# Constants multiplied into the next bank in TensorE's waits, and one-column sums put between dense products

## The reference, cut to what matters

```python
q = q * lax.rsqrt(jnp.sum(q * q, -1, keepdims=True) + L2_EPS)      # the one-column sums
k = k * lax.rsqrt(jnp.sum(k * k, -1, keepdims=True) + L2_EPS)
...
kk = jnp.einsum('bhnik,bhnjk->bhnij', k, k)
sol = lax.linalg.triangular_solve(amat, rhs, left_side=True, lower=True, unit_diagonal=True)
...
o = o * lax.rsqrt(jnp.mean(o * o, -1, keepdims=True) + RMS_EPS) * dn_norm_w * jax.nn.silu(z)   # the tail of a head
...
s = jnp.einsum('bqhgd,bkhd->bhgqk', qb, k, preferred_element_type=jnp.float32) * scale
p = jax.nn.softmax(s, axis=-1)
return jnp.einsum('bhgqk,bkhd->bqhgd', p.astype(v.dtype), v)
...
gu = hn @ w_ffn_in[l]
...
h = h + (jax.nn.silu(g) * u) @ w_ffn_out[l]
```

## Time and profile before

| | us |
|---|---|
| median of 3 runs | 2188.93 (2186.38 to 2196.76) |
| profiled execution | 2186.67 |
| its span | 2184.8 |
| TensorE busy | 1991.2 (91%) |
| VectorE busy | 951.7 (44%) |
| ScalarE busy | 654.0 (30%) |
| GpSimd busy | 434.0 (20%) |
| mean granted clock | 0.945 |

### The profile page before, as it was taken

One profiled execution on the slowest core, in us unless ns is written; L12 is line 12 of the kernel. 1 busy time (PEld: TensorE's weight loads), 2 busy tenths in 40 slices (PEclk: granted clock), 3 DMA queues, 4 the chain that ended last, 5 costly groups with the idle time before them and its releaser, 6 DMA issues.

```text
span 2184.8 us, 22949 instructions
## 1 busy us (share of the span) xinstructions
PE 1991.2 (91%) x9520; PEld 1442.1 (66%) x9520; DVE 951.7 (44%) x1382; ACT 654.0 (30%) x981; POOL 434.0 (20%) x310
## 2 busy tenths in 40 slices
PE   7999989999999889787787889998879899999999
PEld 5887878888877733332333347676746687888787
DVE  7674475542535622110111155845635883222332
ACT  4554422424333101000000133352226753222221
POOL 5432131423326011111110022311003120000121
PEclk9898999999999889898998999999979899999999
DMA  4861423123244589999999953111201134232210
GB/s 164 258 158 49 97 58 78 39 77 57 60 149 182 201 326 405 403 406 407 407 409 411 417 202 116 39 49 49 68 29 39 39 126 154 95 98 98 96 58 39
DMA packets 97654, 361.02 MB, mean 165 GB/s; under 512 B 9850, under 2 KB 34588, under 8 KB 85256
## 3 DMA queue, kind: packets, MB, share of 16 engines
q1 hardware_dynamic: 86800, 335.14, 42.9%
q0 software_dynamic: 8240, 19.00, 2.5%
q10 hardware_dynamic: 2504, 5.35, 0.7%
HBM read 338.74 MB, written 29.10 MB: 168 GB/s over the span
## 4 chain that ended last, share of the span: by engine, by line
PE 78%; DVE 11%; ACT 5%; issue 4%; DMA 1%; POOL 0%; ACTq 0%; SPq 0%; DVEq 0%; POOLq 0%
PE ps L272 74%; PE ps L276 3%; DVE ST L256 2%; PE ps L2080 2%; DVE H L262 1%; ACT ST L268 1%; ACT L268 1%; DVE WL L256 1%; DVE BG L262 1%; DVE ST L994 1%; ACT M L268 1%; DVE sm L3017 0%; DVE BG L256 0%; DMA BG<-h1d,toki 0%; DVE ML L256 0%
## 5 line engine op out<-in xcount | busy, mean ns | idle before, releaser
L272 PE MATMUL ps<-XH,WS 128*128 128x512 f32 x704 | 218.7, 392 | 0.0
L272 PE MATMUL ps<-HTH,WL 128*128 128x512 f32 x448 | 180.0, 402 | 0.0
L272 PE MATMUL ps<-W,BG 128*64 128x512 f32 x496 | 160.2, 618 | 1.0 <-issue 1.0
L272 PEld LDWEIGHTS ps<-XH,WS 128*128 128x128 f32 x704 | 133.5, 190 | 28.1
L2187 DVE COPY BG<-ps 128x512 f32<-128x512 f32 x32 | 22.1, 692 | 288.7 <-PE ps L272 288.7
L266 ACT ACTIVATE BG<-ps 128x512 f32<-128x512 f32 x48 | 28.5, 595 | 373.5 <-PE ps L2080 339.9
L272 PE MATMUL ps<-XL,WS 128*128 128x512 f32 x352 | 138.3, 393 | 1.8 <-DVE XL L256 1.8
L272 PE MATMUL ps<-M,BG 128*64 128x512 f32 (+1 forms) x304 | 125.9, 559 | 7.3 <-ACT ST L266 7.3
L272 PE MATMUL ps<-X2H,GV 128*128 128x512 f32 (+1 forms) x512 | 129.6, 344 | 0.0
L272 PE MATMUL ps<-ST,BG 128*64 128x512 f32 (+2 forms) x416 | 102.5, 597 | 23.5 <-issue 22.7
L272 PE MATMUL ps<-WS,HH 128*128 128x512 f32 x352 | 109.5, 393 | 2.6 <-issue 2.6
(11 more groups left out here) (394 smaller groups left out, 4443.3 us busy)
## 6 DMA issues: line engine op xcount, KB each, us to landing
W<-in_w SPq DMA_DIRECT2D x31, 2048.0 KB, 39.0
W<-in_w_in SPq DMA_DIRECT2D x27, 2048.0 KB, 9.9
ST<-in_w SPq DMA_DIRECT2D x21, 2048.0 KB
BG<-in_w SPq DMA_DIRECT2D x11, 2048.0 KB
U<-in_w SPq DMA_DIRECT2D x11, 2048.0 KB, 33.3
M<-in_w SPq DMA_DIRECT2D x11, 2048.0 KB, 37.8
HT<-in_w SPq DMA_DIRECT2D x11, 2048.0 KB
W<-in_w_ffn_in SPq DMA_DIRECT2D x22, 1024.0 KB, 7.7
```

The lines of the kernel that those rows point to most:

```text
L272: return p.e.matmul(o, lhsT=l, rhs=r, start=start, stop=stop, skip_group_check=True)
```

## The change

It consists of three kinds of edits.

1. A new helper `occupy(t, n)` issues n plain float32 products of constants (`ones` by the first 256 columns of `cst`) into tile t, whose bank has just been waited for. The real products that come next start the tile anew, so that nothing of them is left. It stands after `room(t)` and ahead of the wait for the data, and where the data's wait came first it is moved behind. Calls: 8 at d0, 8 at `x0` of heads 0 and 2, 12 at `p_v2` m=4, 8 at each of granules r6 and s5, 2 at each of the eight turns of attention heads 6 and 7, 5 at the last `p_turn3`, 3 at the first tile of `p_ffn_in`, 4 at the start of `p_ffn_out`: 80 in all.
2. `p_sums` becomes `p_sum(r, y, bank)`, a quarter of it (four products). The quarters stand after d3, d4, d5 (two), d7, d8, d9 (two), and for r=2 and 3 behind k=1 to 4 within d18 and d22.
3. The tail of head h-2 is moved within head h on all engines: the sums on TensorE from behind `kb` to behind `kk`, and into another bank (2 or 5); the scaling from behind `at` to a step behind `eg` (bank 3 or 6); on VectorE each part one step later, and `v_tail` to just ahead of the substitution rows; on ScalarE `s_tail` behind the exponential of `C`.

```diff
+        def occupy(t, n):
+            for _ in range(n):
+                mm(t.at[:, 0:256], ones, cst[:, 0:256])
...
-        def p_dense(n, bank, rhs, kind):
-            p.wait_ge(*split_done(("d", n)))
+        def p_dense(n, bank, rhs, kind, between=()):
             t = B.tile(("d", n), bank, nr=2 if n < 24 else 1)
             room(t)
+            if n == 0:
+                occupy(t, 8)
+            p.wait_ge(*split_done(("d", n)))
             x, hi, lo = parts(("d", n))
...
                 z = exact(t.at, (hi[:, k, :], lo[:, k, :]), (rhs[0][:, k, :], rhs[1][:, k, :]), k == 0, k == 7)
+                if k in between:
+                    p_sum(*between[k])
                 if k == 3:
...
-        def p_sums(r, bank):
-            t = B.tile(("nc", r), bank)
-            room(t)
-            for y in range(4):
-                m = 4 * r + y
-                p.wait_ge(sq_done, m + 1)
-                for i in range(NT):
-                    z = mm(t.at[:, 4 * i + y:4 * i + y + 1], sq_at(m)[:, i * P:(i + 1) * P], ones[:, 0:1])
-            z.then_inc(t.filled)
+        def p_sum(r, y, bank):
+            if y == 0:
+                room(B.tile(("nc", r), bank))
+            t, m = B["nc", r], 4 * r + y
+            p.wait_ge(sq_done, m + 1)
+            for i in range(NT):
+                z = mm(t.at[:, 4 * i + y:4 * i + y + 1], sq_at(m)[:, i * P:(i + 1) * P], ones[:, 0:1])
+            if y == 3:
+                z.then_inc(t.filled)
...
+        SUMS_AFTER = {3: [(0, 0)], 4: [(0, 1)], 5: [(0, 2), (0, 3)], 7: [(1, 0)], 8: [(1, 1)], 9: [(1, 2), (1, 3)]}
         def p_qk():
...
                     p_prep1()
-                    p_sums(0, 6)
                 elif n == 9:
                     p_prep2()
-                    p_sums(1, 7)
+                for r, y in SUMS_AFTER.get(n, ()):
+                    p_sum(r, y, 6 + r)
             p_beta(1, 6)
...
-        def p_turn4(key, bank, x):
+        def p_turn4(key, bank, x, n=0, ready=None):
             t = B.tile(key, bank)
             room(t)
+            if ready:
+                occupy(t, n)
+                p.wait_ge(*ready)
             for c in range(4):
...
             p_spread(("kb", h), b0, h, btr[h // 4])
-            if h > 1:
-                p_tail_sums(h - 2)
             yield
...
             p_products(("kk", h), b0 + 1, lambda c: k4[:, c, :], lambda c: Y[:, c, :])
+            if h > 1:
+                p_tail_sums(h - 2)
             p.wait_ge(gm_done, h + 1)
...
             p_products(("at", h), b0, lambda c: k4[:, c, :], lambda c: q4[:, c, :])
+            yield
+            p_spread(("eg", h), b0 + 2, h, eGr)
+            yield
             if h > 1:
                 p_tail_scale(h - 2)
-            yield
-            p_spread(("eg", h), b0 + 2, h, eGr)
-            yield
             for _ in range(8):
                 yield
-            p.wait_ge(xt0_done, h + 1)
-            p_turn4(("x0", h), b0 + 1, XT)
+            if h == 0 or h == 2:
+                p_turn4(("x0", h), b0 + 1, XT, 8, (xt0_done, h + 1))
+            else:
+                p.wait_ge(xt0_done, h + 1)
+                p_turn4(("x0", h), b0 + 1, XT)
             yield
...
         def p_tail_sums(h):
-            t, z = B.tile(("on", h), 4 + 3 * (h % 2)), sets[h % 2][3]
+            t, z = B.tile(("on", h), 2 + 3 * (h % 2)), sets[h % 2][3]
             room(t)
...
         def p_tail_scale(h):
-            t = B.tile(("os", h), 4 + 3 * (h % 2))
+            t = B.tile(("os", h), 3 + 3 * (h % 2))
             room(t)
...
             tt(v, Y, k4, four(t.at), MUL).then_inc(t.drained)
+            yield
             if h > 1:
                 v_tail_sums(h - 2)
-            yield
-            if h > 1:
-                v_tail_spread(h - 2)
             yield
...
             if h > 1:
-                v_tail(h - 2)
+                v_tail_spread(h - 2)
             yield
...
             yield
+            if h > 1:
+                v_tail(h - 2)
             for i0, i1 in ((1, 5), (5, 8), (8, 10), (10, 12), (12, 14), (14, 15), (15, DB)):
...
             LT, C, X, XT, Y, AT = sets[h % 2]
-            if h > 1:
-                s_tail(h - 2)
             yield
...
             act(C, four(t.at), ACT.Exp).then_inc(t.drained)
-            for _ in range(11):
+            yield
+            if h > 1:
+                s_tail(h - 2)
+            for _ in range(10):
                 yield
...
             for n in range(12, 24):
-                half = p_dense(n, n % 2, hTp, "T")
-                next(half)
-                yield
-                if n == 18 or n == 22:
-                    p_sums(2 if n == 18 else 3, 1)
-                yield from half
+                r = {18: 2, 22: 3}.get(n)
+                yield from p_dense(n, n % 2, hTp, "T", {k: (r, k - 1, 1) for k in range(1, 5)} if r else ())
                 yield
...
             o, w = gr_buf(0), v2_rows(m)
-            x2_ready(m)
-            p.wait_ge(*gr_low(0))
             z = slice(NMETA + m * P, NMETA + (m + 1) * P) if m < 4 else slice(0, NMETA)
...
             room(t)
+            if m == 4:
+                occupy(t, 12)
+            x2_ready(m)
+            p.wait_ge(*gr_low(0))
             for k in range(8):
...
                 o = gr_buf(j)
-                p.wait_ge(*gr_low(j))
                 if kind == "x":
+                    p.wait_ge(*gr_low(j))
                     b = pairs.pop(0)
...
                     room(t)
+                    if (kind, n) in (("r", 6), ("s", 5)):
+                        occupy(t, 8)
+                    p.wait_ge(*gr_low(j))
                     for k in range(8):
...
                 room(u)
+                if h > 5:
+                    occupy(u, 2)
                 p.wait_ge(prob_done[j], 4 * (h // 2) + i + 1)
...
         def p_turn3(i):
-            p.wait_ge(n2_done, i + 1)
             for h in range(2):
...
                 room(t)
+                if i == NT - 1 and h == 0:
+                    occupy(t, 5)
+                p.wait_ge(n2_done, i + 1)
                 for c in range(4):
...
         def p_ffn_in():
-            x3_parts(p)
             for n in range(NF):
-                p.wait_ge(fi_lo, n + 1)
                 o = fi_buf(n)
...
                     room(t)
+                    if n == 0 and y == 0:
+                        occupy(t, 3)
+                        x3_parts(p)
+                    p.wait_ge(fi_lo, n + 1)
                     for k in range(8):
...
             for k in range(NF):
+                if k == 0:
+                    room(acc[0])
+                    occupy(acc[0], 4)
                 p.wait_ge(fh_lo, k + 1)
```

More of the change, by code:

```diff
@@ L1062, in p_head @@
             p_products(("at", h), b0, lambda c: k4[:, c, :], lambda c: q4[:, c, :])
-            if h > 1:
-                p_tail_scale(h - 2)
             yield
@@ L1067, in p_head @@
             yield
+            if h > 1:
+                p_tail_scale(h - 2)
             for _ in range(8):
                 yield
-            p.wait_ge(xt0_done, h + 1)
-            p_turn4(("x0", h), b0 + 1, XT)
+            if h == 0 or h == 2:
[3 more added lines that the diff above has]
+                p_turn4(("x0", h), b0 + 1, XT)
             yield
```

## The result

The changed kernel took 2170.98 us (median of 4 runs, 2163.51 to 2172.85) against 2190.58 for the kernel before; the ratio is 0.9903, 95% interval 0.9879 to 0.9927. Forecast were 2168 us and faster. Its profiled execution took 2172.85, span 2171.0, so the two profiles lie 13.8 us apart where the medians lie 19.6 apart: the profiled execution of before lay 3.9 under its median, that of after 1.9 over its own.

A forecast was written before the change was run, and what follows sets the result against it. TensorE bounds most of the span, losing time at half clock, except where DMA streams the experts' weights. Front -9.2 and behind the experts -11.8 sum to -21.0 us: 2165.7 from the profile, 2168 from the median, range 2161 to 2175.

The forecast's parts named there:

- rival C: All fill sites: fills in waits do not keep the clock, take 0.85 us each, outlast their waits; 2215 us, chance 0.04.
- Net -3.4: Attention heads 6 and 7: clock kept by fills gains 8.4 us, added fills cost 4.3 and 0.75.
- Rival B: Attention heads 6 and 7 stay at 1.2 GHz, fills cost 1.7 each: +11.8 us instead of -3.4; 2183, chance 0.11.
- I take 2.0: Granule r6: fills gain TensorE 2.9 us, but gate sigmoids need VectorE's scan, so 2.0 gained.
- 0.3: Granule s5: same form as r6, with the scan at the end; 0.3 us gained, at most 2.3.
- d0, "0.6": Eight fills fit the 4.40 us wait; products also follow VectorE's low parts, so 0.6 us gained.
- r=0 and r=1: First two blocks of sums, spread among dense products: gains taken as 2.2 and 1.5 us.
- The risk I named: At r=0 and r=1 the last two groups of sums stand together with the preparation step, so the clock may not stay.
- x0 of head 0, "1.2": Fills in the 4.00 us wait gain up to 2.8; TensorE arrives earlier, part stays empty, so 1.2 us taken.
- Rival A's second half: The wait at 173 us is longer than its fills; rival A whole: front gain -3, 2174 us, chance 0.24.
- I take half: Sums at r=3: 2.8 us gained if the clock is held, 0 if not; 1.3 taken.
- -3.3 ... +1.2 +0.6 +0.8: Moved tail: 3.3 us gained before head 4; VectorE price 1.2 at heads 4, 5, 0.6 at 6, 7, 0.8 at 2, 3.

The follow-up runs named there:

- the thin fills: The whole change with each of the 80 fills cut from 256 to 16 columns; 2178.27 us, 0.9954 of the kernel before.
- its repeat: The changed kernel itself run once more, nothing altered; 2168.55 us, 0.9907 of the kernel before.
- the second profile of before: The kernel before, unchanged, profiled again; 2181.31 us in one run.
- the one pair of traces that reach attention together: Changed kernel without d0, r6, s5 fills, sum quarters each alone, 6 fills at head 0's x0: with attention fills 2166.65 us, without 2168.8.

## Why the prediction was right, and by which steps it was not

The forecast of 2168 and the range held, but by luck: two wrong sizes cancelled, the fills put too high and the tail too low. By medians the parts are nearly additive:

| part | forecast | part alone | taken out of the whole |
|---|---|---|---|
| 80 fills | -15.3 | -6.6 | 7.0 |
| sums | -5.0 | -3.9 (without fills, less tail alone) | 7.8 |
| tail | -0.7 | -9.7 | 7.8 |
| all | -21.0 | -20.3 | measured -19.6, -20.7 |

Each measured entry is a difference of medians and uncertain by 3 to 5 us; the two wrong sizes lie outside that, the two entries of the sums within it.

Right, in mechanism and size: the fills at v2, at the last turn and first feed-forward tile, at the output product (-6.1 forecast, -5.9 in after's profile); kb within 0.6; that constants of 256 columns hold the clock in a wait that they fill (rival C fell, by the thin fills too). x0 of head 2 came out at the forecast 0.9 by two errors that cancelled: the fills gave 0.9 to 1.0 with the tail moved or not, instead of 1.7, and the tail's price of 0.8 there did not show. That nothing won ahead of the experts is lost in them is not settled: after and its repeat stood as far ahead of the first profile of before at 1262 as at 700, to 0.25, but the second profile of before had by then gained 3.5 on the first.

- **Attention, "Net -3.4".** The mechanism was right, the added 0.86 too: the two turns among dense products lost 1.7 between 1600 and 1605, and the rounds show 1.16 for scores and 4.75 for the ten-record product, as forecast. Mis-sized was what it is compared with. In before the clock was back by itself for some of the scores and turns, and in which ones varies: without them the stretch gave between +0.6 and -3.7. Measured worth of the fills in the one pair of traces that reach attention together: 0.1. Rival B did not come: with the fills the clock was 0.94, with one half-clock stretch at 1610. The Trainium skill says ("TensorE: Matmul & The Clock Gate", section "Part 4: PE-mode transpose") that transposes do not count as TensorE being busy in the way other matmuls do. No run here separates the transposes; turns and scores without fills ran at 0.64, which does not contradict it.
- **r6 and s5, "I take 2.0" and "0.3".** TensorE did gain 2.7 at r6, and by 1720 the lead was smaller than at 1700: the next granule waits 1.77 for its low half from VectorE (1710.95 above). I had named the scan as what is late next; the low split at the granule behind it was later. What was kept was won at s5. The stretch gains 1.5 to 1.9 in five profiles without these fills too, but these five had lost 1.6 just ahead, to a half-clock stretch at 1680 that before does not have. From 1640 to 1750 together, all seven profiles without these fills gain or lose under 0.3; with them, three without the fall at 1680 gained 1.6 to 2.2 and three with it 0 to 0.6. So they are worth about 1 on the mean, not 2.3. No kernel leaves them out alone, and why the clock falls at 1680 in eight profiles of fourteen is open: after shows no fall there, its repeat does.
- **d0, "0.6".** The fills kept the clock for the first products, TensorE then ran ahead of the low halves, waited 2.11 and came out of that wait at half clock (29.14). The wait had moved, not gone: +1.3 in four of six profiles, where the seven without fills stand at -0.3 to -0.45.
- **r=0 and r=1.** The risk I named came about: two quarters with the preparation step (1.95 in one piece; 1.85 behind a 1.36 wait for a square) let the clock fall near 70 in every profile and at 97 in all but one. -1.5 and +0.3. Not even the 1.5 is surely the edit's: of the five profiles with the sums in a block two stand at -1.6. With each quarter by itself 45 to 75 gave 3.1.
- **x0 of head 0, "1.2".** Rival A's second half: the fills ended at 170.1, the wait went on for 3.24, the clock fell. Nothing gained.
- **r=3, "I take half".** 3.1 in eight of nine profiles, and 0 in all that keep the block: all that I had put at the stretch (2.8). This is the clearest gain of the sums.
- **The tail, "-3.3 ... +1.2 +0.6 +0.8".** kb was right at -3.5. The price on VectorE was 0.85 at heads 4 and 5, and nothing shows at the others. And the step left out the same block at 528, which in the profile I read had kept its clock; it costs 3.3 when it falls. Two profiles of four are too few for a rate. With a half of 3.3 the tail is worth 4.3 by places; the medians say 7.8 and 9.7. Where the remaining 3 to 5 us lie stays open: no profile shows them in one place, and the two profiles of before differ by 5.4 with nothing edited. So the failed size is known by the medians, and its cause only for the half.

## What to carry to other kernels

In this kernel a block of one-column products or row spreads was often followed by half clock. Spreading it helped where dense products stood between the single pieces (r=3, the tail) and not where two pieces stood together or one was preceded by a wait (r=0, r=1); try it before filling waits, since it adds no instructions. Constants multiplied in a wait paid where the wait had a fixed end and one row of them reached to just ahead of it (v2, both feed-forward places); between many short waits they cost about what they brought. And count every place where a harmful pattern stands, not only those where the one profile at hand shows the harm. Last, a total that comes out right says nothing of its terms: only the kernels with parts left out showed that two of them were wrong.

## What the runs showed of the hardware

The half-clock stretches of one kernel are not the same in each execution. Half-clock time per run, as twice one less the mean granted clock times the span, was 223 to 259 us over 17 runs of before and 138 to 165 over six of after. The same block of one-column products led to a half-clock stretch of 6.8 us in one profile of before and 3.4 in the other. That alone moves a step read from one profile by 1.6 us, and of the run-to-run spread of a kernel (2183 to 2198 us over 17 runs of before) it may be much.

Where nothing is edited it can be seen with the work held equal. In attention, from 1498.67 in before and from 1492.12 in after, both traces show the same records at the same distances for 11.5 us at full clock. Then the clock of after is half from 1503.8 to 1507.2, that of before is not, and after loses 1.5. Eleven of the fourteen profiles lose 1.5 or 3.1 between 1460 and 1515; the two of before and the one without fills lose nothing. So the work just ahead of a fall doesn't settle whether it comes. What does is not shown. And the gain by clock was not the gain in time: fills took the median half-clock time of the change without them from 209 to 156, worth 26 us if every one counted, and the time by 7.
